# Turning 24 normalised tiles and all attention results with transposing DMAs instead of TensorE, in a decoder layer on one Trainium2 chip

## The reference, cut to what matters

```
h    = rmsnorm(x) @ w_in                    # -> q | k | v | u, 512 channels each
q, k = rope(q), rope(k)                     # 8 heads of 64
y_a  = softmax(q k^T / 8, masked) @ v       # own block of 256 keys (causal) + top-3 earlier blocks
y_p  = pool_mixer(u)                        # trailing means over 2, 4, 8, 16 tokens, a linear map
x    = x + rmsnorm([y_a | y_p] @ w_out)
a    = rmsnorm(x) @ w_up                    # 5632 channels
a    = causal_conv3(a) + b;  gate, val = halves of a
x    = x + rmsnorm((silu(gate) * val) @ w_down)
```

## Time and profile before

| what | value |
|---|---|
| median of 3 runs | 801.34 us (800.68 to 801.72) |
| the profiled execution, time | 800.46 us |
| the profiled execution, span of the slowest core | 798.9 us |
| spans of the 8 cores | 797.5 to 798.9 us |
| granted TensorE clock, mean by core | 0.996 to 0.998 of full |
| busy: PE / DVE / ACT / POOL | 757.9 / 471.3 / 408.0 / 282.7 us |

### The profile page before, as it was taken

How to read it: one execution, slowest core, us unless ns; L and a number is a source line. 1 busy time by engine, 2 the same in 40 slices (tenths; PEclk the granted TensorE clock), 3 DMA queues, 4 the chain that set the end, 5 groups by cost and what they waited for, 6 DMA issues and landing times.

```text
span 798.9 us, 15004 instructions; the slowest of 8 cores (797.5 to 798.9 us)
## 1 busy us (share of the span) xinstructions
PE 757.9 (95%) x4891; PEld 388.2 (49%) x4980; DVE 471.3 (59%) x682; ACT 408.0 (51%) x669; POOL 282.7 (35%) x312
## 2 busy tenths in 40 slices
PE   2899999999999999999999999999999999999995
PEld 1376545555565655444444444444444444444442
DVE  4767677545453444777687874242677777772222
ACT  6477415668899999454464442111354444541111
POOL 1442353220333444355665455010244444331000
PEclk9999999999999999999999999999999999999998
DMA  8996521116238234747878668063444444001321
GB/s 260 322 274 170 167 87 42 37 27 110 80 96 174 106 107 158 132 90 136 158 141 163 118 112 140 1 210 121 117 80 80 79 80 80 1 0 56 124 85 53
DMA packets 31052, 91.36 MB, mean 114 GB/s; under 512 B 3968, under 2 KB 9856, under 8 KB 29952
## 3 DMA queue, kind: packets, MB, share of 16 engines
q0 software_dynamic: 12688, 32.77, 25.0%
q1 hardware_dynamic: 18288, 57.62, 22.1%
HBM read 100.99 MB, written 16.78 MB: 147 GB/s over the span
## 4 chain that ended last, share of the span: by engine, by line
PE 89%; issue 3%; DVE 3%; ACT 2%; DMA 2%; SPq 0%; DVEq 0%; POOLq 0%; ACTq 0%; POOL 0%
PE ps L871 37%; PE ps L954 19%; PE ps L754 8%; PE ps L691 6%; PE ps L596 6%; PE ps L822 6%; PE ps L772 4%; DMA MEM<-w_qk 2%; PE ps L573 1%; PE ps L759 1%; ACT MEM L768 1%; DVE MEM L521 1%; PE ps L719 1%; ACT MEM L881 0%; DVE MEM L603 0%
## 5 line engine op out<-in xcount | busy, mean ns | idle before, releaser
L871 PE MATMUL ps<-MEM 128*128 128x512 bf16 x1378 | 305.6, 379 | 3.4 <-DVE MEM L891 1.2
L871 PEld LDWEIGHTS ps<-MEM 128*128 128x128 bf16 x1408 | 137.2, 98 | 165.9 <-issue 3.3
L881 ACT ACTIVATE MEM<-ps,MEM 128x1024 f32<-128x1024 f32 x88 | 105.9, 1203 | 142.0 <-PE ps L871 138.1
L768 ACT ACTIVATE MEM<-ps 128x512 bf16<-128x512 f32 (+1 forms) x320 | 150.5, 554 | 48.2 <-PE ps L759 23.1
L954 PE MATMUL ps<-MEM 128*128 128x512 bf16 x689 | 151.3, 379 | 0.8
L907 POOL TENSOR_TENSOR MEM<-MEM 128x1024 bf16<-128x1024 f32 x44 | 103.5, 2352 | 119.6 <-DVE MEM L894 81.0
L884 DVE SCALAR_TENSOR_TENSOR MEM<-ps,MEM 128x1023 f32<-128x1023 f32 x88 | 112.8, 1281 | 55.2 <-ACT MEM L881 54.8
L887 DVE SCALAR_TENSOR_TENSOR MEM<-ps,MEM 128x1022 f32<-128x1022 f32 x88 | 112.7, 1281 | 8.1
L954 PEld LDWEIGHTS ps<-MEM 128*128 128x128 bf16 x704 | 68.9, 98 | 83.1
L754 PE MATMUL ps<-MEM 72*128 72x512 bf16 (+1 forms) x320 | 102.0, 348 | 3.4 <-ACT MEM L768 1.7
L543 POOL TENSOR_SCALAR MEM<-MEM 128x1 f32<-128x1 f32 x63 | 12.9, 205 | 226.0 <-ACT MEM L962 118.8
(11 more groups left out here) (89 smaller groups left out, 651.9 us busy)
## 6 DMA issues: line engine op xcount, KB each, us to landing
MEM<-w_up_r POOLq DMA_DIRECT2D x44, 512.0 KB, 6.9
MEM<-x SPq DMA_DIRECT2D x32, 512.0 KB, 4.8
x1s<-MEM SPq DMA_DIRECT2D x16, 512.0 KB, 3.6
MEM<-x1s SPq DMA_DIRECT2D x16, 512.0 KB, 4.5
out<-MEM SPq DMA_DIRECT2D x15, 512.0 KB, 2.6
MEM<-w_down POOLq DMA_DIRECT2D x22, 256.0 KB, 8.1
MEM<-w_qk SPq DMA_DIRECT2D x4, 1024.0 KB, 15.4
MEM<-w_vu SPq DMA_DIRECT2D x4, 1024.0 KB, 20.5
```

Of the source, the lines that this page charges most:

```text
L768: op("act", lambda e, c0=c0, u=u, p=p: e.activation(out=PT[p][:, c0:512], in_=bk[u.ids[0]][:, c0:512], func=AF.Exp, scale=SCALE), rd=u.b, ...
L871: mm = op("pe", lambda e, c=c, half=half, pr=pr, ws=ws, tb=tb: e.matmul(bk[pr.ids[tb]], lhsT=wu[ws][:, c, half * 128:(half + 1) * 128], rh ...
L881: op("act", lambda e, pr=pr, ch=ch, ts=ts: e.activation(out=tA[ts], in_=ps(pr)[:, :], func=AF.Identity, scale=cwb[:, ch, 2:3], bias=cwb[:, ...
```

## The change: what it does

The helper `dma` gets a flag `turn`, with which it issues `dma_start_transpose` in place of `dma_start`. The planner gets a cost for such a DMA. Three users of PE transposes are switched, all on SP's queue:

- first-norm tiles 8 to 15 (groups 2 and 3): a new `turned` instead of `transposes`, one DMA of 128x1024 bf16 (256 KB) from `xn` into `HY`;
- the second-norm tiles 0 to 15 in `sec1`: the same;
- the attention result of each pair of heads: one DMA of 128x512 bf16 (128 KB) from `yb[k]` into `HY`.

First-norm tiles 0 to 7 are turned by PE as before. The evictions of the switched transposes go with them, since a DMA writes `HY` directly.

```
-    def dma(self, queue, key, pairs, rd=(), wr=(), wp=(), deps=(), nbytes=524288, cast=False, prio=None):
+    def dma(self, queue, key, pairs, rd=(), wr=(), wp=(), deps=(), nbytes=524288, cast=False, prio=None, turn=False):
...
-        fn = lambda e: [e.dma_start(out=o_, in_=i_) for (o_, i_) in pairs]
+        fn = lambda e: [e.dma_start_transpose(out=o_, in_=i_) if turn else e.dma_start(out=o_, in_=i_) for (o_, i_) in pairs]
...
-                if busy and o["nbytes"] < 200000:
+                if o["turn"]:
+                    line[e] = max(line[e], t + 1.2) + o["nbytes"] / (0.5 * rate)
+                    fin = max(line[e], free_at[e]) + 4.0
+                elif busy and o["nbytes"] < 200000:
...
+            if tt >= 8:
+                return lambda: turned(tt, xb, hT_b[tt], xi)
             return lambda: transposes(tt, xb, hT_b[tt], xi, 0.0 if tt < 4 else 0.8)
+
+        def turned(tt, xb, dst_b, xi):
+            dma("sp", "xt%d" % xi, [(HY[:, :, tt * 128:(tt + 1) * 128], xn[xi])], rd=[xb], wr=[dst_b], nbytes=262144, turn=True)
...
                     if r == 1:
-                        tu = Use([(3,), (2,), (1,), (0,)])
-                        for qb in range(4):
-                            op("pe", lambda e, qb=qb, k=k, tu=tu: e.transpose(
-                                out=bkh[tu.ids[0]][:, qb * 128:qb * 128 + 128], in_=yb[k][:, qb, :], identity=ident),
-                               rd=[ybb, buf("cst")], n=128, slack=0.3, **W(qb == 0, tu.b[0]))
-                        dst = HY[:, h // 2, G * 512:(G + 1) * 512]
...
-                        sc.either(dict(act=lambda e, dst=dst, src=src: e.copy(out=dst, in_=src()),
-                                       dve=lambda e, dst=dst, src=src: e.tensor_copy(out=dst, in_=src())),
-                                  512, dict(dve="x2"), rd=tu.b, wp=[yT_b[G]])
+                        dma("sp", "yt%d" % k, [(HY[:, h // 2, G * 512:(G + 1) * 512].rearrange("p (q n) -> p q n", q=4),
+                                                yb[k].rearrange("p q n -> p (q n)"))],
+                            rd=[ybb], wp=[yT_b[G]], nbytes=131072, turn=True)
...
-            transposes(tt, xb, hT2_b[tt], tt % 2, 1.0)
+            turned(tt, xb, hT2_b[tt], tt % 2)
```

More of the change, by code:

```diff
@@ L159, in dma @@
             self.dsem[key] = [self.st.enter_context(self.nc.semaphore("d_" + key)), 0]
-        fn = lambda e: [e.dma_start(out=o_, in_=i_) for (o_, i_) in pairs]
-        o = dict(kind="dma", key=key, sig=False, seq=0, slack=0.0, ndma=len(pairs), nbytes=nbytes, cast=cast,
+        fn = lambda e: [e.dma_start_transpose(out=o_, in_=i_) if turn else e.dma_start(out=o_, in_=i_) for (o_, i_) in pairs]
+        o = dict(kind="dma", key=key, turn=turn, sig=False, seq=0, slack=0.0, ndma=len(pairs), nbytes=nbytes, cast=cast,
                  alts={queue: (fn, (0.62 if queue == "pool" else 0.45) * len(pairs), 0.0)})
@@ L793, in attn @@
                     if r == 1:
-                        tu = Use([(3,), (2,), (1,), (0,)])
-                        for qb in range(4):
-                            op("pe", lambda e, qb=qb, k=k, tu=tu: e.transpose(
-                                out=bkh[tu.ids[0]][:, qb * 128:qb * 128 + 128], in_=yb[k][:, qb, :], identity=ident),
-                               rd=[ybb, buf("cst")], n=128, slack=0.3, **W(qb == 0, tu.b[0]))
-                        dst = HY[:, h // 2, G * 512:(G + 1) * 512]
-                        def src(tu=tu):
-                            return bkh[tu.ids[0]][:, 0:512]
-                        sc.either(dict(act=lambda e, dst=dst, src=src: e.copy(out=dst, in_=src()),
-                                       dve=lambda e, dst=dst, src=src: e.tensor_copy(out=dst, in_=src())),
-                                  512, dict(dve="x2"), rd=tu.b, wp=[yT_b[G]])
+                        dma("sp", "yt%d" % k, [(HY[:, h // 2, G * 512:(G + 1) * 512].rearrange("p (q n) -> p q n", q=4),
+                                                yb[k].rearrange("p q n -> p (q n)"))],
+                            rd=[ybb], wp=[yT_b[G]], nbytes=131072, turn=True)
         x1w = [None] * NT
```

## The result

The changed kernel takes 792.12 us (three of its four runs 791.48 to 792.39) against 801.05 us before (800.68 to 801.72): a ratio of 0.9885 with a 95% interval of 0.9866 to 0.9904, or 8.9 us less. The forecast was 790.0 with a range of 783 to 808.

What follows compares the result with a forecast made beforehand. PE's queue, busy 95% of the span, was taken to bound the kernel. -14.1 + 1.5 + 2.5 - 1.0 = -11.1 us from 800.46 gave 789.4, 790 with the median's 0.9 us; range 783 to 808.

Steps and rivals of the forecast that it cites:

- PE's transposes, -14.1 us: PE's queue: 256 transposes removed at 0.055 us each, read from eight in a full queue, save 14.1 us.
- ACT at its limit, +1.5 us: 200 to 320 us: ACT, busy 112 of 114.3 us, gives back 1.5 us of the 5.7 gained, bounds 0 and 5.7.
- waits, +2.5 us: First-norm tiles 8 to 15: ACT's and PE's waits for late tiles, delayed key and query copies included, 2.5 us, between 0 and 7.
- The end of attention, -1.0 us: From 320 us on: 1 us of PE's 3.6 idle gained by placing up-projection matmuls earlier, bounds 0 to 3.
- The landing of the last attention result, 5.3 us under 12.8 of cover: Last attention result: lands after 5.3 us, hidden by 58 matmuls of line 869, 12.8 us, before its reader.
- the prediction's own signs: Profile after: landing of 10 us or more, PE or ACT waiting at group 2, or late weights would make the forecast wrong.
- Ring time, 90 us: DMA rings: 32,768 packets at 44 ns take 90 us; by bytes alone 26, at the far bound of 154 ns 315.
- landing of a tile: Turned tiles: land after 2.5 us fixed plus 2.8 on the rings, 5.3 us; far bounds 3.3 and 12.4.
- Slower by late tiles: Rival, norm of tiles 8 to 15: landing of 12.4 us leaves 20 us of waits, 809 us; chance 0.22.
- ACT taking over: Rival, 200 to 320 us: ACT keeps all 5.7 us and tile waits are 5 us, 798 us; chance 0.13.
- SP's order holding keys and queries: Rival, attention groups 2 and 3: SP's queue delays key and query copies 5 us each, 800 us; chance 0.08.
- the larger gain: Rival, whole kernel: nothing is lost to ACT or waits, -14.1 - 3 gives 784 us; chance 0.12.

Runs made afterwards that it cites:

- run 10: Changed kernel, but three up-projection weight loads issued beside the last attention result wait until it has landed; 859.12 us against 859.1 for the changed kernel on chip 1.
- run 5: The changed kernel itself again, on the second chip; 796.76 us against 807.5 for the kernel before, ratio 0.9875.
- run 7: Changed kernel with plain copies of the same bytes in place of the transposing DMAs, tiles not turned, second chip; 794.33 us, ratio 0.9826.
- Run 6: Changed kernel, but the last attention result is turned by four PE transposes, second chip; 794.52 us, ratio 0.9842.
- run 1: Changed kernel, but all 16 attention results are turned by PE again, tiles by DMA, chip 1; 855.55 us against 862.84 for the kernel before.
- run 9: The changed kernel itself again, on chip 1; 859.1 us against 863.39 for the kernel before.
- run 2: Changed kernel, but all tiles are turned by PE again, only the 16 attention results by DMA, chip 1; 865.47 us, no faster than the kernel before.
- run 11: Changed kernel, but first-norm tiles 8 to 15 and the last attention result are turned by PE again, chip 1; 861.33 us.

## Why the prediction was right, and where it was off

**PE's transposes, -14.1 us: right.** On core 5, summing the stretches of both traces, PE's busy time fell from 762.8 to 747.3 us, -15.5, or 0.061 us for each of 256 against the 0.055 read from eight in a full queue. The idle time read from the earlier trace rows was too large, since that core's trace lacks 89 matmul records: core 5 was idle 2.8 us, not 3.6, from 320 to 420 us.

**ACT at its limit, +1.5 us, and waits, +2.5 us, between 60 and 320 us: right in sum, not in kind.** PE's idle time there rose on core 5 from 4.5 to 7.4 us, 3.0 against 4.0. ACT, at 114 of 120 us, has 1.0 us of it (the scores' waits for exponentials are 1.7 against 0.7 us); the short waits at the pooling matmuls and behind them have 2.4 us against 0.2 before, in an order that I had not read. A wait for tiles 8 to 15, for which the 2.5 us were set, is on no core; the only DMA waits of PE from 60 to 320 us are 0.2 to 1.1 us at the scores, line 762, on six cores. ACT did not reach the 97% that was to be seen from 200 us on; it was busy 115.2 and 114.1 of 120 us.

**The end of attention, -1.0 us: small.** Idle time from 320 to 420 us fell by 2.8 us on core 5 (97.22 to 100.00 busy), near the bound of 3. With the rest, an undisturbed core gets 15.2 us, not 11.1.

**The landing of the last attention result, 5.3 us under 12.8 of cover: wrong.** "If that cover were gone, PE would wait those 5.3 us once": the cover was there, 58 matmuls and 13.0 us on core 1 (316.86 to 329.85), and the landing was 8.5 to 16.0. The step that failed took the landing from the copy's fixed 2.5 us plus ring time. Alone it is even less: 2.4 to 2.6 us for a result in run 10, 3.1 to 3.3 for single tiles in the changed kernel. The sum misses what runs beside it. The earlier trace rows had shown 7.9 us beside other traffic, and I charged it to the copies of keys and queries, not to this one. Three casting loads from GpSimd's queue start within 5 us of it, and they were to be seen in the trace of before. By the prediction's own signs a landing of 10 us or more would have made the forecast wrong; it came, twice in the span, and the time was right all the same, because few readers stand that close.

**Its price: mis-sized by the clock.** A wait of 2.3 us cost 3.9, since about eight of the matmuls behind it ran at the lower level. The two falls of the clock, 1.5 and 1.7 us on core 1, are in no term, nor is its 1.4 us before 60 us. That the forecast came within 2.1 us of the time is in part luck: the terms were 4 us too careful for an undisturbed core, and the slowest core lost 7 us that no term held. The range and the direction rest on the transposes, which were priced rightly.

**Ring time, 90 us, and landing of a tile: right side, both taken too high.** SP's queue went from 176.6 to 0.306 x 790.3 = 241.8 us of all engines: 65 us for 34,048 more packets, 31 ns each against 44 taken and a far bound of 154. The lower bound by bytes alone, 26 us, is excluded too. The median landing on core 1 is 4.1 us.

**The two pages.** The Trainium skill (VectorE: DVE Perf Modes, The three transpose paths) gives 1309 ns for a transposing DMA of one block, by which, as an estimate, eight in turn would take 10.5 us; tiles of eight blocks land whole in 3.1 to 3.3 us when alone, so the measurement speaks against that reading. Another page of the Trainium skill (Advanced Engine Details and Errata, X-Bar Transpose (TRN2)) has them as fast as ordinary ones. Alone the trace agrees in the landing, 2.4 to 2.6 us against 2.9 for a copy of 128 KB in the kernel before; beside casting loads it does not: 10.2 to 15.5 us (run 5) against 5.9 to 9.0 for a copy of the same bytes (run 7).

**The rivals.** Slower by late tiles: 20 us of waits in front of group 2 were not there. ACT taking over and SP's order holding keys and queries: the scores wait for a copy of keys or queries for 1.1 us at most, although these copies now land after 4.2 to 5.3 us instead of 2.9. So that mechanism exists, at a fifth of its forecast size. Five of the eight cores, with spans of 783.1 to 785.2 us, came near what the larger gain forecast: 784 us of time, or a span of about 782.4 with the 1.6 us around it.

**What the evidence leaves.** Run 6 is the best measured version that computes the same: 0.9842 (0.9824 to 0.9859) beside 0.9875 (0.9841 to 0.9909) for the changed kernel on the same chip. That it beats the change is likely and not shown. On chip 1, run 1 has the lowest median of those that compute the same, 855.55 us, 7.3 under the kernel before beside it where run 9 is 4.3 under; the clocks of that chip don't allow ranking them. What the late last result costs the whole kernel is therefore open: one core's trace shows 3.9 us, and no run that removed it is faster beyond its interval.

## What to carry to other kernels

Price a transposing DMA twice: alone, and beside what else is in flight when it is issued, above all loads that cast. Give the last one of a chain, which has a reader at once, to another engine or keep the loads away from it for 3 us. On several cores, look at the spread of the spans: a wait of 2.3 us of TensorE on one core cost 3.9 with the clock, and the slowest core sets the time. Before busy times are compared, see that both traces have all their matmul records. And where a planner orders the work, read the new order as a change of its own: each edit here moved something else by 1 to 3 us.

## What the runs showed of the hardware

- A transposing DMA of 128 KB within SBUF lands after 2.4 to 2.6 us with no casting load beside it (eight cores, run 10) and after 8.5 to 16.0 us with two or three of 512 KB beside it in the change and run 9; another one, issued at 233 to 236 us behind three loads, after 10.8 to 14.2 us in the change. A plain copy of the same bytes beside the loads lands after 5.9 to 9.0 us (run 7).
- Other small copies suffer: those of keys and queries, 128 KB, land after 4.2 to 5.3 us in the median of a core instead of 2.8 to 3.0, and the scores wait up to 1.1 us for them in the change and 2.5 in run 1.
- Turning costs packets: 34,048 more on the queue where plain copies of the same bytes are 27,264, at 31 and 23 ns each ((0.272 x 792.7 - 176.6) x 16 / 27,264 for the second).
- After waits of TensorE of 2.3 to 4.0 us, with matmuls in a row before and behind, its clock fell to the lower level for some microseconds in 16 of 27 cases: behind the wait for the last result on 3 of 3 cores in the change (2.3, 2.5 and 3.2 us), 2 of 3 in run 5, 2 of 2 in run 9 and 3 of 7 in run 2, behind the wait for VectorE on 2 of 8 in run 10 (2.7 to 2.9 us), at 258 to 263 us on 3 of 3 in run 11, and at 95 us on 1 core in run 1. Waits of 2.0 and 2.2 us in run 9 were followed by a fall as well. With waits for the last result of 1.2 to 1.9 us it did not fall. What decides is open.
- The DMA engines can be 94 to 98% busy over 60 us with TensorE at 99% (60 to 120 us in the change).
